# Decay gates computed inside the input projection; second norm inside the out-projection; third norm and router inside the cross-attention's projection; last expert visit inside the loop

## Reference

```python
h = rms_norm(x, norm_mix_g)                     # x: 1024 tokens x 1024
q, k, v, r, gf, gb, glu = split(h @ w_in)       # 2592 columns; gf, gb: 16 each
la_f = log_sigmoid(gf @ w2_f + b_f) / 16        # decay gates, 256 columns, per direction
la_b = log_sigmoid(gb @ w2_b + b_b) / 16
o = gla(q, k, v, la_f) + flipped gla(..., la_b) # cumulated decays, per-head norm, swish(r)
b_out = silu(layer_norm(conv31(glu)))
x = x + concat(o, b_out) @ w_out
x = x + cross_attention(rms_norm(x), rms_norm(mem))   # wq, 256 memory tokens, wo
h = rms_norm(x)
logits = h @ router_w + router_b                # 32 experts, top 4
x = x + moe(h)                                  # clamped SwiGLU experts, 1024 x 2048, 1024 x 1024
y = rms_norm(x)
```

## Time and profile before

| | us |
|---|---|
| median of 3 runs | 2657.73 |
| profiled execution | 2655.09 |
| its span | 2653.3 |
| PE busy | 2399.1 (90%) |
| DVE busy | 1814.8 (68%) |
| ACT busy | 1286.2 (48%) |
| POOL busy | 366.5 (14%) |
| mean granted PE clock | 0.947 |

### The profile page before, as it was taken

The page is one execution under the profiler, slowest core; times in us unless marked ns, Lnnn a source line. Parts: engine busy times, 40 slices in busy tenths (PEclk is TensorE's granted clock), DMA queues, the critical chain, the costliest instruction groups (busy, mean ns, idle before and its releaser), DMA issues.

```text
span 2653.3 us, 38454 instructions
## 1 busy us (share of the span) xinstructions
PE 2399.1 (90%) x13540; PEld 1952.5 (74%) x13605; DVE 1814.8 (68%) x1880; ACT 1286.2 (48%) x1418; POOL 366.5 (14%) x305
## 2 busy tenths in 40 slices
PE   6999785698978977899999999999999999999983
PEld 5889574497846975777777777787787777777762
DVE  4499588614043157788977787778777778988763
ACT  4212455403132124656755565566555556766543
POOL 0000000010000042122211211122122112222210
PEclk9999896698999959899999999999999999999996
DMA  3111210311100028989987897789787789999764
GB/s 137 48 48 49 80 34 17 124 45 32 48 16 1 11 103 295 322 305 321 367 292 252 262 317 252 232 280 327 258 279 244 240 296 315 345 363 311 251 220 147
DMA packets 263104, 523.03 MB, mean 197 GB/s; under 512 B 10812, under 2 KB 44912, under 8 KB 262928
## 3 DMA queue, kind: packets, MB, share of 16 engines
q1 hardware_dynamic: 246112, 466.30, 49.8%
q0 software_dynamic: 15008, 52.70, 8.5%
q10 hardware_dynamic: 1904, 2.90, 0.4%
HBM read 482.27 MB, written 39.58 MB: 197 GB/s over the span
## 4 chain that ended last, share of the span: by engine, by line
PE 76%; DVE 12%; issue 5%; ACT 5%; DMA 1%; DVEq 1%; ACTq 0%; POOL 0%; POOLq 0%
PE PS L2347 12%; PE PS L2349 11%; PE PS L2348 11%; PE PS L1946 9%; PE PS L2355 7%; PE PS L2352 6%; PE PS L2166 4%; PE PS L2232 3%; DVE wlo L1740 2%; PE PS L2317 1%; PE PS L2219 1%; ACT whi L1014 1%; PE PS L2184 1%; PE PS L2186 1%; PE PS L2185 1%
## 5 line engine op out<-in xcount | busy, mean ns | idle before, releaser
L1740 DVE TENSOR_TENSOR wlo<-raw,whi 128x2048 fp32r<-128x2048 f32 x387 | 878.9, 2287 | 208.9 <-ACT whi L1014 179.9
L1014 ACT CAST whi<-raw 128x2048 fp32r<-128x2048 f32 x387 | 731.1, 1911 | 189.6 <-PE PS L2355 137.3
L2347 PE MATMUL PS<-whi,xhi 128*128 128x512 f32 x1024 | 426.2, 416 | 33.4 <-DVE yb L1823 17.5
L2349 PE MATMUL PS<-whi,xlo 128*128 128x512 f32 x1024 | 402.3, 393 | 0.0
L2348 PE MATMUL PS<-wlo,xhi 128*128 128x512 f32 x1024 | 400.4, 391 | 0.0
L2349 PEld LDWEIGHTS PS<-whi,xlo 128*128 128x128 f32 x1024 | 193.2, 189 | 42.6
L2348 PEld LDWEIGHTS PS<-wlo,xhi 128*128 128x128 f32 x1024 | 193.8, 189 | 39.0
L2347 PEld LDWEIGHTS PS<-whi,xhi 128*128 128x128 f32 x1024 | 194.8, 190 | 37.6 <-DVE wlo L1740 3.3
L2347 PE MATMUL PS<-whi,hhi 128*128 128x512 f32 x512 | 203.2, 397 | 21.1 <-DVE wlo L1740 21.1
L2349 PE MATMUL PS<-whi,hlo 128*128 128x512 f32 x512 | 200.0, 391 | 0.0
L2348 PE MATMUL PS<-wlo,hhi 128*128 128x512 f32 x512 | 199.9, 390 | 0.0
(11 more groups left out here) (395 smaller groups left out, 4560.8 us busy)
## 6 DMA issues: line engine op xcount, KB each, us to landing
raw<-in_exp_w_up SPq DMA_DIRECT2D x259, 1024.0 KB, 6.2
raw<-in_exp_w_down SPq DMA_DIRECT2D x128, 1024.0 KB, 6.8
ring<-in_w_in SPq DMA_DIRECT2D x11, 1024.0 KB, 5.3
xres<-in_x SPq DMA_DIRECT2D x4, 1024.0 KB, 10.0
ring<-in_xattn_wk SPq DMA_DIRECT2D x4, 1024.0 KB, 7.6
ring<-in_xattn_wv SPq DMA_DIRECT2D x4, 1024.0 KB, 5.0
ring<-in_w_out SPq DMA_DIRECT2D x4, 1024.0 KB, 7.0
xres<-in_x SPq DMA_DIRECT2D x1, 4096.0 KB, 18.8
```

The source lines that it names most:

```text
L1014: nc.scalar.copy(whi[:, chunk_slot(c, NSPL), :], raw[chunk_slot(c, NRAW)][:]).then_inc(s_whi, 1)
L1740: nc.vector.tensor_tensor(wlo[:, chunk_slot(c, NSPL), :], raw[chunk_slot(c, NRAW)][:], whi[:, chunk_slot(c, NSPL), :].bitcast(F), ALU.subtract
L2347: pe.matmul(o, hi[:, k, :], wh, start=first and bias is None, stop=False)
L2349: ins = pe.matmul(o, lo[:, k, :], wh, start=False, stop=stop and kk == 3)
```

## The change

Eight parts. (1) PE's eight gate products move behind chunk 0 of the input projection; ACT copies them to `Zg`, runs both softplus passes there, DVE both cumulations. The results are stored to DRAM (`decay_scratch`) and reloaded into `Bf` and `Rb` before each pair. (2) Memory chunk 0 moves between LayerNorm's two sums; `scores(0, 0)` comes ahead of memory chunk 1. (3) The second norm works tile by tile: mean, root, scale, turn, cast and low part follow the residual add of each tile in c = 3; banks 4 to 7 take the turns. (4) The q-projection takes its first chunk's groups in the order that begins with tokens 0 to 511, and turns 6 and 7 lie between them. (5) The third norm and the router are interleaved with the last eight groups of the attention's projection in the same way. (6) `EARLY_BASE` is 8, and SP stores four tiles, loads expert chunks 8 and 9, then stores the other four. (7) The last visit's rest is an Else branch inside the loop on all five engines. (8) Placement in SBUF follows.

```diff
-EARLY_BASE = 6
+EARLY_BASE = 8
...
-        used = ([("in", n) for n in (2, 6, 10, 14, 18, 22, 26, 34, 42, 54, 62)]
+        used = ([("in", n) for n in (2, 14, 18, 22, 26, 30, 34, 42, 50, 62, 70)]
...
+        def out_bank(n):
+            return PS[:, n % 8 if n < 3 * TT else n % 4, 0:256]
+        def o_bank(n):
+            return PS[:, n % 8 if n < 3 * TT else n % 2, 0:256]
...
+            def reload_decays(p):
+                if p == 0:
+                    sp.wait_ge(s_spill, 2 * 16)
+                for i, to in enumerate((Bf, Rb)):
+                    sp.dma_start(to[:], br_dram[p, :, i, :]).then_inc(s_rel, 16)
...
+                if g == N_IN + 1:
+                    reload_decays(0)
                 if g == g_out:
+                    sp.wait_ge(s_ex, exps_of(0, "starts") + 2)
+                    reload_decays(1)
                     sp.wait_ge(s_ket, 8)
...
+                if g == 3:
+                    for p in range(2):
+                        sp.wait_ge(s_rb, 2 * p + 2)
+                        sp.dma_start(br_dram[p], BR[p][:]).then_inc(s_spill, 16)
...
+            sp.wait_ge(s_h3s, 16 * TT)
             for c in range(4, 8):
                 load_chunk(0, c, e0, None, fresh=True)
...
+            store_base(range(TT // 2))
+            sp.wait_ge(s_acc, 16 * (TT // 2))
             for c in range(8, 4 + NRAW):
                 load_chunk(0, c, e0, None, fresh=True)
+            store_base(range(TT // 2, TT))
...
+            for p in range(2):
+                for d in range(2):
+                    for th in range(2):
+                        done = drain("in", n)
+                        nc.scalar.copy(Zg[p][:, d, 512 * th:512 * (th + 1)], bank_groups(n)).then_inc(done, 1)
+                        n += 1
+            softplus(0)
+            softplus(1)
...
-            softplus(1)
             window_decays(1)
...
+            y_square(0)
+            for t in range(1, TT):
+                y_square(t)
+                y_root(t - 1)
+                if t >= 4:
+                    hidden_states_hi(t - 4)
...
+            z_square(0)
+            for t in range(1, TT):
+                z_square(t)
+                z_root(t - 1)
+                if t >= 4:
+                    h3_turned_out(t - 4)
+            z_root(TT - 1)
             act.wait_ge(s_mm["o"], 32)
...
+            gate_minima(0)
+            w_in_lo(2)
+            cumulated(0)
+            gate_minima(1)
+            w_in_lo(3)
+            cumulated(1)
             glu_tile(0)
...
-            gate_minima(0)
-            cumulated(0)
+            dve.wait_ge(s_rel, 2 * 16)
             exponents(0)
...
-            gate_minima(1)
             empty_states(0)
             states(0, 0, 14)
...
-            cumulated(1)
-            exponents_to_ends()
+            dve.wait_ge(s_rel, 4 * 16)
+            exponents_to_ends(1)
...
+            for t in range(TT + 4):
+                if t < TT:
+                    add_residual("out", 3 * TT + t, out_bank)
+                if t == 1:
+                    wq_lo(0)
+                if 1 <= t <= TT:
+                    y_mean(t - 1)
+                if 2 <= t <= TT + 1:
+                    y_scale(t - 2)
+                if t >= 4:
+                    hidden_states_lo(t - 4)
...
+            for t in range(TT + 5):
+                if t < TT:
+                    add_residual("o", 3 * TT + t, o_bank)
+                if 1 <= t <= TT:
+                    z_mean(t - 1)
+                if 2 <= t <= TT + 1:
+                    z_scale(t - 2)
+                if t >= 5:
+                    logits(t - 5)
...
-            with dve.Fori(1, NVIS) as t:
+            with dve.Fori(1, NVIS + 1) as t:
                 with dve.If(t <= last_):
...
+                with dve.Else():
+                    with dve.If(t <= last_ + 1):
+                        both_last = has_tail(last_)
+                        for c in range(15, 19):
+                            lo_by_vector(last_, c)
+                        tail_rows(last_ + 1, both_last, low=1)
...
+            pe.wait_ge(s_dr["in"], 2)
+            for p in range(2):
+                for d in range(2):
+                    for th in range(2):
+                        if n == 6:
+                            pe.wait_ge(s_pvc, 2)
+                        if n >= 8:
+                            pe.wait_ge(s_dr["in"], n - 7)
+                        pe.matmul(bank_groups(n), W2[:, d, P * p:P * (p + 1)], gT[:, 512 * th:512 * (th + 1)],
+                                  start=True, stop=True).then_inc(s_mm["in"], 1)
+                        n += 1
...
+            memory_chunk(0)
             pe.wait_ge(s_lna, CT)
...
-            gates(0)
-            memory_chunk(0)
+            scores(0, 0)
             memory_chunk(1)
-            scores(0, 0)
...
+                    if n >= 27:
+                        turn_y(n - 27)
...
             pe.wait_ge(s_dr["out"], 32)
-            norm_turn("y", TT)
+            turn_y(5)
+            pe.wait_ge(NY["drained"], TT)
...
+                    if n in (1, 2):
+                        turn_y(5 + n)
+                    if n == 2:
+                        pe.wait_ge(NY["drained"], 2 * TT)
...
+                    if n >= 27:
+                        turn_z(n - 27)
+                    if n >= 28:
+                        router(n - 28)
...
+            turn_z(5)
+            router(4)
+            turn_z(6)
+            router(5)
+            turn_z(7)
+            router(6)
+            router(7)
```

More of the change, by code:

```diff
@@ L480, in _ @@
                         load_chunk(t + 1, c, en, ed)
-            e_last = expert(last_)
-            for c in range(15, 19):
-                load_chunk(last_, c, None, e_last, last=True)
+                with sp.Else():
+                    with sp.If(t <= last_ + 1):
+                        e_last = expert(last_)
+                        for c in range(15, 19):
+                            load_chunk(last_, c, None, e_last, last=True)
             wait_multiplied(sp, last_, 14)
@@ L608, in _ @@
                     scatter(t - 1)
-            scatter(last_)
+                with pool.Else():
+                    with pool.If(t <= last_ + 1):
+                        scatter(last_)
         @block.scalar
@@ L915, in split_wq @@
                 if c == 1:
-                    act.wait_ge(norms["y"]["turned"], 2 * TT)
+                    act.wait_ge(s_mm["out"], 4 * TT)
                 if c >= 2:
@@ L1521, in _ @@
             dve.wait_ge(s_xre, 32)
-            add_residual("out")
+            for n in range(3 * TT):
+                add_residual("out", n, out_bank)
             def wq_lo(c):
@@ L1539, in _ @@
-            wq_lo(0)
-            split_norm("y", gxb, 2, hidden_states_lo)
+                    turned = PS[:, 4 + 2 * (t % 2) + b, :].rearrange("p (k c) -> p k c", k=4)
+                    for i, (k0, k1) in enumerate(((0, 2), (2, 4)) if b == 0 else ((0, 4),)):
+                        ins = nc.vector.tensor_tensor(hL[2 * b + i][:, :, cols], turned[:, k0:k1],
+                                                      hH[:, 4 * b + k0:4 * b + k1, cols].bitcast(F), ALU.subtract)
+                    ins.then_inc(NY["drained"], 1)
@@ L2027, in _ @@
             pe.wait_ge(s_lnv, 10)
-            def gates(p):
-                for i in range(4):
-                    d, th = i // 2, i % 2
-                    pe.matmul(PS[:, i, :], W2[:, d, P * p:P * (p + 1)], gT[:, 512 * th:512 * (th + 1)],
-                              start=True, stop=True).then_inc(s_z, 1)
             def scores(p, l):
                 L = 8 * p + l
-                if l == 0:
-                    pe.wait_ge(s_zmin, 4 * (p + 1))
-                    pe.wait_ge(s_zabs, 4 * (p + 1))
-                else:
+                if l:
                     pe.wait_ge(s_kq, products_of(p, l - 1))
@@ L2150, in _, with turn_y @@
             pe.wait_ge(s_yl, 2)
+            NY = norms["y"]
+            def turn_y(t):
+                pe.wait_ge(NY["scaled"], t + 1)
+                if t < 2:
+                    pe.wait_ge(s_dr["out"], 3 * TT)
+                else:
+                    pe.wait_ge(NY["drained"], 2 * (t - 1))
+                for b in range(2):
+                    for k in range(4):
+                        ins = pe.transpose(PS[:, 4 + 2 * (t % 2) + b, P * k:P * (k + 1)],
+                                           XNy[t % 2][:, P * (4 * b + k):P * (4 * b + k + 1)], ident[:])
+                    ins.then_inc(NY["turned"], 1)
             for c in range(4):
@@ L2158, in _ @@
                     if n >= 8:
-                        pe.wait_ge(s_dr["out"], n - 7)
+                        pe.wait_ge(s_dr["out"], n - 7 if n < 28 else n - 3)
                     tile = slice(P * t, P * (t + 1))
@@ L2422, in _ @@
                     pe.wait_ge(s_hlo, t)
-            down(last_ + 1, pe.snap(tail_last, min_val=0, max_val=1), c0=3, read=0)
+                with pe.Else():
+                    with pe.If(t <= last_ + 1):
```

(1 more changed line is left out.)

380 lines of the change are left out of this document (198 added, 182 removed).

## The result

| | before | after |
|---|---|---|
| median, 8 runs each | 2651.89 us | 2635.13 us |
| lowest and highest | 2644.96, 2658.10 | 2631.40, 2640.72 |
| ratio, 95% interval | | 0.9943, 0.9930 to 0.9957 |
| span of the profiled execution | 2653.3 us | 2630.2 us |

The change makes the kernel 16.8 us faster, 0.6%. The forecast was 40 us. It set out from 2657.7 us, the median of three runs of the kernel before; that of all eight is 2651.9. Read stage by stage, the two profiles (one of each kernel) give this account. A stage ends at the start of the named instruction; minus is a gain.

What follows compares the result with a forecast made beforehand. PE was taken to bound the input projection and expert loop, with valleys between dense products. Terms -14.7 - 10 - 4 - 1.5 - 11 + 1 = -40.2 from 2655.1 gave 2614.9, plus 2.6: 2617 us; own range 2600 to 2634, with rivals 2594 to 2642.

Steps and rivals of the forecast that it cites:

- Gates, paid first: Input projection: wait for gT 2.1 us plus eight gate products move it back by 9.2 us; stores and reloads cost 0.
- eight such took 7.13 us at full clock: Input projection: duration taken for the eight 512-column fp32 gate products on PE, 7.13 us.
- Gates, taken back: LayerNorm and pair 0: -10.8, then +1 for PE's cold restart; pair 1: -14.1. With the 9.2 paid, -14.7.
- rival 2: Gates give little back: conv or reloads late, or pair 0 tied to LayerNorm; -4 instead of -14.7, 2628 us, chance 0.12.
- Second norm: Out-projection to q-projection: PE's idle or turning stretch falls from 24.5 to 15.7 us; -10 taken, ends -14 and -4.
- Third norm and router: Interleaved with the o-projection's last groups: last logits at 966 instead of 971.47; -4, ends -13 and +17.
- Groups 28 to 30 each bring 5 us: O-projection's last groups: each adds 3.3 us waiting for ACT's copies plus 1.65 us router; last group 16 us late.
- rival 1: Third norm's valley stays cold into the o-projection, each group at half clock: +21, 2638 us, chance 0.13.
- Start of the experts: First visit: two waited-for loads come early, -1.5, ends -6 and 0; the gather through DRAM sets the start anyway.
- Last visit: Last down products: PE starts 12 us earlier; empty iterations move beside scatter and reload; -11, ends -12.5 and -7.
- Loop jumps: Expert loop: one more jump per engine in 31 real visits, +1, ends 0 and +64.
- Rival 3: Loop ends: each visit's jump over the epilogue makes PE wait up to 2.06 us, 64 us in all; 2680, chance 0.04.

Runs made afterwards that it cites:

- Run 5: Changed kernel with the eight gate products contracted over 128 rows instead of 32, the added rows zeros; ratio 0.9922 to the kernel before.
- run 12: Run 8's kernel plus gate products over 128 rows and ACT's down-bias loads issued behind the second of four last third-norm copies; ratio 0.9765, median 2588.20 us.
- run 13: Run 12's kernel with third norm and router behind the whole o-projection again, edits that have no place there gone; ratio 0.9839, median 2612.71 us.
- run 3: Changed kernel with ACT copying the turned third-norm tile out ahead of the next tile's squares; ratio 0.9890 to the kernel before.
- run 8: Changed kernel with POOL's bias steps early, DVE's router-load wait later, ACT's copies first, loops ending at the last visit; ratio 0.9817 to the kernel before.
- run 1: Changed kernel with POOL's splitting of the experts' up biases moved ahead, beside the o-projection; ratio 0.9873 to the kernel before.
- run 4: Changed kernel with its fifth part undone: third norm and router behind the whole o-projection again; ratio 0.9885 to the kernel before.
- run 9: Kernel before the change, with only POOL's bias steps held until DVE's first routing step; ratio 1.0069 to the kernel before.

## Why the prediction was wrong, step by step

**Gates, paid first.** The wait, the two shifts, the cover of the convolution and the stores and reloads held: DVE's taps ended in time, no chunk came late. The step that failed is "eight such took 7.13 us at full clock". It took the duration from products with 128 rows for products with 32, and with them 12.28 us and the cold start of chunk 1 came: 15.0 instead of 9.2. Run 5 shows that the rows did it: nothing but the rows (and where gT lies) differs, and the products take 7.13 us; runs 12 and 13 have it too. With 32 rows they took 11.1 to 14.0 us in nine profiles.

**Gates, taken back.** -10.7 for LayerNorm and pair 0 against -9.8, and -14.2 for pair 1 against -14.1. Right in mechanism and size; rival 2 did not happen.

**Second norm.** -12.7 against -10, within its ends. It was not tried by itself, and the kernel before took 206.3 to 210.2 us for this stretch in four profiles, so the 2.7 us are not told from none.

**Third norm and router.** This step failed: "Groups 28 to 30 each bring 5 us" has the right chain (group, addition, square, copies, router) and two thirds of its price, which was 7.9 us (10.76 less a group of 2.9). That chain is idle time of PE, and idle time was charged at the full clock, with a margin of 1.3 us. It cost the clock as well: rival 1's mechanism, at 10.8 us a tile instead of 12.3. The Trainium skill ("TensorE: Matmul & The Clock Gate", PE-mode transpose) says that turns do not count as busy in the same way, so that the full clock does not come with them. In run 12 the clock was 1.00 from 906 to 917, with turns and small router products alone, and in run 3 over 23 us with turns between the groups, so this case does not show a fall by that rule. The pauses were what mattered: in the seven profiles that keep them a tile took 7.7 to 10.8 us, and in the three without (runs 3, 8 and 12) 5.5 us at a clock of 1.00. DVE's wait for loads that were now wanted earlier was missing from the sum too; PE lost some 0.4 us by it.

**Start of the experts.** "The gather sets the start anyway" was right, since the first up product follows it by 14.8 us in both kernels. The step that failed is what routing was put at, nothing: -1.5 was wrong by 13 us, for a reason not in the sum: POOL's work, which I had not listed among the queues that the norm was moved past. It did not wait and was not waited for; it only ran at another time. Runs 1, 4 and 9 show it from three sides.

**Last visit.** PE started 12.4 us earlier as forecast. "ACT just fits and DVE is 0 to 2 us late" failed: an empty pass costs ACT 17.03/21 = 0.81 us with the nested comparison, not the 0.6 taken, and the tail gave 4 us back. **Loop jumps** cost some 3 us, not 1. The Trainium skill ("Advanced Engine Details and Errata", Control Flow Timing) gave 51 ns a jump and so an estimated 1.6 us. The traces have about 0.1 us a visit, twice that. Rival 3 had the right place and, at 2.06 us, a price far too high.

In all, of the 17 us between the traces' 23.1 and the forecast 40.2: 5.8 gate products, 5.5 third norm, 13.1 routing, 3.6 tail, less 11 of terms that came out better, of which pair 1's clock is the largest. That the time, 2635, lay in the range is in part luck: the starting value fell by 5.8 us with more runs, and of the four losses only the third norm's was among the rivals that the range was made for.

## What to carry to other kernels

When a stage is moved earlier, list not only who waits for it but what else runs at its new time, POOL's work on SBUF above all: nothing in the program says that two engines hold each other up, and only the durations show it. An experiment that moves a line moves its queue too, and a profile is one execution: compare a stage that the edit can't touch as well. Price a pause of TensorE among short products twice, once as the pause and once as the half clock that may come behind it, and put the instruction that the next product waits for at the head of its engine's queue. Bound a loop by the number of real iterations where that can be had: here it beat both arrangements of the empty ones.

## What the hardware did that I had not expected

- Products with 32 rows brought the clock from 2.4 to 1.2 GHz with PE busy throughout (0.50 over 53.5 to 64); the same products over 128 rows, mostly zeros, held 1.00.
- DVE's two-input steps on SBUF stood still while POOL's casts and subtractions ran: 0.45 us became 2.7 on average in the changed kernel, 0.19 became 3.47 in run 9, with reductions and reciprocals between them unchanged. A cast with one input (0.20 to 0.79 us, at 944.08 in the changed kernel) stood as well, while the additions of 0.42 us beside POOL's memset in run 9 (965.97 to 967.77) kept their time.
- The clock's return is not a fixed matter: the same 96 value products took from 12.4 to 18.5 us in four executions of the kernel before, which is a third of what this change was worth.
